# Two weight items of each expert mixture in borrowed memory, and experts laid out by quarters of columns

## What is computed

```python
# first block: 32 experts of width 512, each token has two of them
for e in range(N_EXPERTS):
    h = jax.nn.silu(t @ w_gate[e]) * (t @ w_up[e])
    y = y + combine[:, e:e + 1] * (h @ w_down[e]).astype(jnp.float32)
...
# second block, both layers: 16 experts of width 1024, each takes its 32 best tokens
cap = EC_CAPACITY_FACTOR * n // N_EXPERTS_2
aff = jax.nn.softmax(h.astype(jnp.float32) @ w_router.astype(jnp.float32), axis=-1)
g, idx = lax.top_k(aff.swapaxes(1, 2), cap)
xs = jax.vmap(lambda hb, ib: hb[ib])(h, idx)
a = jax.nn.silu(jnp.einsum('becd,edf->becf', xs, w_gate)) * jnp.einsum('becd,edf->becf', xs, w_up)
y = jnp.einsum('becf,efd->becd', a, w_down) * g[..., None].astype(h.dtype)
...
# around each mixture of the second block
sh_m, sc_m, g_m, sh_f, sc_f, g_f = ada_params(c, ada_w[l], ada_b[l])
x = x + g_m * y
x = x + g_f * ec_moe(modulate(x, norm_ffn[l], sh_f, sc_f), ...)
```

## Time and profile before

| | us |
|---|---|
| median of 3 runs | 2042.81 (2042.49 to 2046.18) |
| the profiled execution | 2041.44 |
| its span, first to last instruction | 2039.4 |
| PE busy | 1616.9 (79%) |
| DVE, ACT, POOL busy | 562.9, 298.1, 88.1 |
| transferred | 711.34 MB, mean 349 GB/s |

### The profile page before, as it was taken

How to read it: one execution, slowest core, us unless ns; L and a number is a source line. 1 busy time by engine, 2 the same in 40 slices (tenths; PEclk the granted TensorE clock), 3 DMA queues, 4 the chain that set the end, 5 groups by cost and what they waited for, 6 DMA issues and landing times.

```text
span 2039.4 us, 21810 instructions
## 1 busy us (share of the span) xinstructions
PE 1616.9 (79%) x8868; PEld 755.1 (37%) x8868; DVE 562.9 (28%) x1055; ACT 298.1 (15%) x707; POOL 88.1 (4%) x102
## 2 busy tenths in 40 slices
PE   7999788888888798896676867666997677767767
PEld 3455544433334244664231313112874132313212
DVE  3753311111111177744111101112653111101101
ACT  2123211111111111332010101001001110100000
POOL 2210000000000052000000000000000000000000
PEclk9989799999999899897888988988997898888988
DMA  9532499999999966434999999999973999999997
GB/s 364 202 128 73 191 422 419 422 421 424 422 422 422 406 232 238 174 145 164 421 419 420 423 420 420 424 420 407 377 298 124 421 420 425 420 420 422 423 421 317
DMA packets 118364, 711.34 MB, mean 349 GB/s; under 512 B 5763, under 2 KB 8067, under 8 KB 93571
## 3 DMA queue, kind: packets, MB, share of 16 engines
...
HBM read 709.03 MB, written 1.05 MB: 348 GB/s over the span
## 4 chain that ended last, share of the span: by engine, by line
DMA 48%; PE 37%; DVE 6%; issue 4%; ACT 3%; POOL 2%; POOLq 0%; ACTq 0%; DVEq 0%
DMA ring<-in_moe_w_down 39%; DMA ring<-in_w_down 8%; PE bank L1475 7%; PE bank L459 4%; PE bank L1430 4%; PE bank L2229 4%; PE bank L1499 4%; PE bank L1348 4%; PE bank L900 1%; PE bank L603 1%; PE bank L2007 1%; POOL small L255 1%; DVE gate_rows L371 1%; DVE ada_acc L371 1%; PE bank L314 1%
## 5 line engine op out<-in xcount | busy, mean ns | idle before, releaser
L1430 PE MATMUL bank<-ring,arena 128*32 128x512 f32 x3072 | 401.8, 651 | 143.3 <-DMA ring<-in_moe_w_up 100.9
L1475 PE MATMUL bank<-ring,arena 128*32 128x512 f32 x1536 | 230.9, 728 | 160.7 <-DMA ring<-in_moe_w_down 121.2
L1499 PE MATMUL bank<-arena 128*128 128x512 f32 x512 | 236.3, 604 | 28.2 <-DVE arena L1554 16.1
L1521 DVE COPY arena<-bank 128x512 f32<-128x512 f32 x96 | 66.4, 691 | 666.0 <-PE bank L1430 666.0
L1430 PEld LDWEIGHTS bank<-ring,arena 128*32 128x32 f32 x3072 | 93.6, 114 | 378.9 <-issue 251.7
L459 PE MATMUL bank<-ring,hT 128*128 128x512 f32 (+1 forms) x352 | 158.6, 602 | 1.6 <-DVE hT L329 1.6
L1475 PEld LDWEIGHTS bank<-ring,arena 128*32 128x32 f32 x1536 | 50.5, 121 | 293.7 <-issue 183.0
L1513 ACT ACTIVATE arena<-bank 128x512 f32<-128x512 f32 x96 | 57.3, 597 | 615.4 <-PE bank L1430 615.4
L1499 PEld LDWEIGHTS bank<-arena 128*128 128x128 f32 x512 | 92.8, 191 | 136.8 <-issue 95.1
L1348 PEld LDWEIGHTS bank<-arena,xn 128*128 128x128 f32 x512 | 124.5, 335 | 8.3 <-DVE arena L1380 3.7
L1348 PE MATMUL bank<-arena,xn 128*128 128x128 f32 x512 | 123.5, 404 | 3.3 <-DVE arena L1380 3.3
...
## 6 DMA issues: line engine op xcount, KB each, us to landing
...
```

The costliest lines, as they stand in the source:

```text
L1430: last = nc.tensor.matmul(AA[hf if M.nf == 2 else up][32 * j:32 * j + 32, :], xgT[:, x + kk, a:a + C], w[:, kq + j, hf * NC:(hf + 1) * NC] ...
L1475: last = nc.tensor.matmul(AA[n][32 * j:32 * j + 32, :], act_s[:, b, q * C:(q + 1) * C], w[:, j, n * NC:(n + 1) * NC], start=(kk < 4), stop ...
L1499: nc.tensor.matmul(Y[2 * t + n][:, :], wselT[:, e % 2, t * P:(t + 1) * P], z_s[:, n * NC:(n + 1) * NC], start=(e == 0 and M.fresh), stop=( ...
L1521: v.tensor_copy((up_s if up else gate_s)[:, a:a + NC], AA[1][:, :]).then_inc(M.u_dve if up else M.g_dve, 1)
```

## The change

- **Lent memory.** Items 4 and 7 of each mixture no longer go to the ring. Item 4 goes to `arena[:, 8192:12288]`, item 7 to the whole of `gate_rows`, each 2 MB. SP waits for the last users of that memory in the dense part (`lent_free`). The ring places of the other items shift down. To make room, `ctxT` moves to `gate_rows`, the gate of the mixtures becomes `gate_strips` (256 columns on four groups of 32 partitions), and some small tiles move.
- **The context** is prepared at the end of M1, at experts 28 to 30 (loads, squares, scale, turns, evacuation by ACT and DVE), in `gate_rows`, instead of in block 1.
- **Quarters of columns.** In M2's gate and up, and in all down products, quarter j of the array now takes 256 of the 1024 output columns and the whole contraction. The items of M2 need 16 matmuls of 256 columns instead of 8 of 512. Copies and sums of gate and up are gone in M2; silu and product read PSUM. z is 256 columns wide. M1's gate and up stay as they were.
- **Return by row groups.** `back_pe` has 8 matmuls of 32 contraction rows and 256 columns, in two halves of four on four row groups and four banks, with a wait between the halves.
- **Gather** goes over four banks; from the second group on it also waits for the product and the turned weights of the expert before.
- **Flag.** It is read ahead of the last four experts of M1 on PE, ACT, DVE; the branch stays behind M1.
- Gate loads from `ada_b`: one of 512 KB at the start of block 2 and of the odd layer each, and 4 small ones (128 KB together) at the start of block 1 and of the odd layer, in place of four of 512 KB.

```diff
+HEAD = 8192
+QW = D // 4
+LENT = (4, 7)
...
-    items += [("moe",)] * (3 * E1)
+    items += [("moe", i) for i in range(3 * E1) if i not in LENT]
...
+            if sec % 6 == G_F:
+                for j in range(4):
+                    last = nc.tensor.matmul(banks[0][32 * j:32 * j + 32, 0:QW], const("ones")[:, 0:C], acc[:, j * QW:(j + 1) * QW],
+                                            start=True, stop=True)
...
         def ctx_load_act():
-            nc.scalar.wait_ge(at_v, 16)
+            nc.scalar.wait_ge(M1.done, M1.done0 + LENT[1] + 1)
...
         def gather_pe(M, k, g, r):
+            if g:
+                pe.wait_ge(M.act, nth(M, GE * g - 1, 1, r, k))
+                pe.wait_ge(M.wT, nth(M, GE * g - 1, 1, r, k))
             for kk in range(KD):
-                if kk >= 2:
-                    pe.wait_ge(M.xg_dve if kk % 2 else M.xg_act, nth_group(M, 4 * g + kk // 2, 4, r, k))
+                if kk >= 4:
+                    pe.wait_ge(M.xg_dve if kk % 2 else M.xg_act, nth_group(M, 4 * g + kk // 2 - 1, 4, r, k))
                 for t in range(T):
-                    last = nc.tensor.matmul(AA[kk % 2][:, 0:GE * C], xn[:, t, kk::KD], sel[:, b * T + t, :], start=(t == 0), stop=(t == T - 1))
+                    last = nc.tensor.matmul(XG[kk % 4][:, 0:GE * C], xn[:, t, kk::KD], sel[:, b * T + t, :], start=(t == 0), stop=(t == T - 1))
...
-                            kk = n * part + kq + j
-                            last = nc.tensor.matmul(AA[hf if M.nf == 2 else up][32 * j:32 * j + 32, :], xgT[:, x + kk, a:a + C],
-                                                    w[:, kq + j, hf * NC:(hf + 1) * NC], start=(kk < 4), stop=(kk >= 4))
+                            last = nc.tensor.matmul(GU[up][32 * j:32 * j + 32, 0:QW], xgT[:, x + kk, a:a + C],
+                                                    w[:, kq, j * QW:(j + 1) * QW], start=(kk == 0), stop=(kk == KD - 1))
...
         def down_pe(M, k, e, r):
-                        last = nc.tensor.matmul(AA[n][32 * j:32 * j + 32, :], act_s[:, b, q * C:(q + 1) * C],
-                                                w[:, j, n * NC:(n + 1) * NC], start=(kk < 4), stop=(kk >= nk - 4))
+                        last = nc.tensor.matmul(z_bank(M)[32 * j:32 * j + 32, 0:QW], act_s[:, b, q * C:(q + 1) * C],
+                                                w[:, kq, j * QW:(j + 1) * QW], start=(kk == 0), stop=(kk == nk - 1))
...
         def back_pe(M, k, e, r):
-            for t in range(T):
-                for n in range(2):
-                    nc.tensor.matmul(Y[2 * t + n][:, :], wselT[:, e % 2, t * P:(t + 1) * P], z_s[:, n * NC:(n + 1) * NC],
-                                     start=(e == 0 and M.fresh), stop=(e == M.ne - 1 and M.gate is not None)).then_inc(M.y, 1)
+            for n, order in enumerate((((0, 0), (0, 2), (1, 1), (1, 3)), ((0, 1), (0, 3), (1, 0), (1, 2)))):
+                if n:
+                    pe.wait_ge(M.y, nth(M, 8 * e + 4, 8, r, k))
+                for t, j in order:
+                    rows_, at = slice(32 * j, 32 * j + 32), (j % 2) * QW
+                    nc.tensor.matmul(Y[2 * t + j // 2][:, at:at + QW], wselT[rows_, e % 2, t * P:(t + 1) * P], z_s[rows_, :],
...
             def put(i, rows_):
                 free(M, k, i, r, looped)
+                if i in M.lent:
+                    n = M.lent.index(i)
+                    nc.sync.dma_start(lent[n].rearrange("p (k n) -> p k n", n=rows_.shape[2]), rows_).then_inc(lent_arrived[n], 16)
+                    return
...
+        def lent_free(stage, n):
+            if stage == 1:
+                return [(at_m, 24), (ada_sums, 4)] if n else [(at_q, 4), (at_v, len(att1))]
+            if stage == 2:
+                return [(out_added, 8)] if n else [(a2_o, 4), (a2_v, len(att2)), (fourier_steps, FY_MM)]
+            return [(out_added, 12)] if n else [(ada_sums, 13)]
```

392 lines of the change are left out of this document (220 added, 172 removed).

## The result

Median 2021.56 us (2020.46 to 2025.22, four runs) against 2044.10 (2042.49 to 2046.18, four runs) of the kernel before: ratio 0.9892, interval 0.9875 to 0.9909. The change gives 22 us where I forecast 42, and the time lies 6.6 us above the upper end of my range. The profiled execution is 2021.36 us with a span of 2019.5.

A forecast was written before the change was run, and what follows sets the result against it. Mixtures were taken as bound by weight transfers not started ahead, dense parts by PE, DVE and small-step chains. From 2041.44 us, -29.8 - 5.4 + 2.5 - 5.5 - 2.5 - 1.0 = -41.7 gave 1999.7, stated as 2001; range 1991 to 2015.

The forecast's parts named there:

- M1's end: From expert 30's down to block 2's first matmul: 17.65 us before, 10.7 to 12.4 forecast; gain taken as 5.5.
- first gathers: Each mixture's first gather, on the path: four banks instead of two save 1.8 us each, 5.4 over three.
- M2[0]'s end: From 1400.31 to the norm: 16.9 us before, 16.5 or 14.8 forecast; gain taken as 1.0.
- context load: Context loads moved into M1's stream of transfers: 1.05 MB at 422 GB/s, 2.5 us lost.
- M2[1]'s end: From expert 14's down to the last addition's end: 18.9 us before, 17.9 or 16.2 forecast; gain taken as 1.5.
- Lending: Two more items transferred ahead of each of three mixtures, 9.94 us each: 29.8 us gained.
- no gain in the middle: M2's items by quarters of columns: 1.93 us of PE each, under the transfers' 5.0, so nothing changes.
- My bound of 0: Lower bound of a first gather's gain (upper 3.9 us): nothing saved if all of it runs at the low clock.
- 3 if the issue stays: At M1's end, the gain is only 3 us if the branch's 3.35 us of issue does not shrink to 1.
- Dense parts: Outside the mixtures: cheaper gate sums gain about 2 us, ACT's issue of five transfers loses 1; together 1 gained.
- Rival 2: Only the transfers gain: PE at low clock, row groups one after another, gathers stay 7.9 us; 2014 us, chance 0.12.

The follow-up runs named there:

- e1: The changed kernel with no item lent, all of a mixture's items through the ring of five: 2051.33 us, ratio 1.0035 to the kernel before.
- e2: The changed kernel with both M2's gate, up and down matmuls issued as before, half as many, numbers not the reference's: 2017.01 us, ratio 0.9870.
- e5: The changed kernel with the gather's weights read from neighbouring columns instead of every eighth, so other features than the reference's: 2014.95 us, ratio 0.9873.
- e12: The changed kernel with the gather over two banks as before, all else as changed: 2022.29 us, ratio 0.9898.
- e14: The changed kernel with ScalarE writing the normed rows a second time by feature, and the gather on neighbouring columns: 2012.69 us, ratio 0.9855.
- e15: The changed kernel with matmuls that keep TensorE busy in its waits and later odd-layer gate loads, the gather's weights still strided: 2013.27 us, ratio 0.9858.
- e8: The changed kernel loading 16 columns of each context row instead of 1024, so block 2's values differ from the reference's: 2024.53 us, ratio 0.9921.
- e4: The changed kernel without the block of further M1 passes for experts with more than 32 tokens; the flag's load stays: 2015.49 us, ratio 0.9861.
- e6: The changed kernel with matmuls only keeping TensorE busy in each mixture's last expert and behind M2[0]'s last return: 2022.38 us, ratio 0.9901.
- e3: The kernel before with do-nothing TensorE instructions added in both M2, which were absent from the program that ran: 2044.04 us, ratio 1.0005.

## Why the prediction was wrong, point by point

On the profiled executions I forecast 41.7 us and got 20.1. The 21.6 us that are missing lie in these steps: instruction fetches, which had no term, 7.2 (0.8 of it not shown); M1's end 5.5; the first gathers 5.4; M2[0]'s end 2.3; the context load 1.0; the lent items 0.8; and M2[1]'s end gave 0.8 more than forecast.

- **Lending**, -29.8: right, -29.0 by e1, or -27.0 if the longer distance in e1's M1 is taken off. SP was in time in all three.
- **Quarters of columns, "no gain in the middle"**: this is the step that failed most, in size and in its reasoning. I costed 32 against 16 instructions an item in PE's time, found 1.93 us under 4.97 and took it as free. That is what it is for PE. But the instructions themselves come through the DMA engines, the one resource that was full: 3.1 and 3.3 us in the two M2 (e2). In M1 I put it at some 0.8, the distance at the end of 4.0 instead of 3.2, with 14 fetches instead of 11; other traces with 14 end at 3.2 to 4.2, so this 0.8 is not shown.
- **First gathers**, -5.4: 0. I read 0.96 us a step as the round trip over two banks at the full clock. It was the strided weight loads (e5, e12, e14). The row to see it by stood in the page of before too, below: 335 ns a load (second row), where other loads of 128 x 128 fp32, those of the return, took 191. That the loads are as busy as the matmuls would not have told it, since they are in e14 too (65.4 and 68.4 us). My bound of 0 was for another reason, the low clock, and that was the second limit (e14, e15).

```profile
L1499 PEld LDWEIGHTS bank<-arena 128*128 128x128 f32 x512 | 92.8, 191 | 136.8 <-issue 95.1
L1348 PEld LDWEIGHTS bank<-arena,xn 128*128 128x128 f32 x512 | 124.5, 335 | 8.3 <-DVE arena L1380 3.7
```

- **Context load**, +2.5: the mechanism right, the size 3.5 (e8).
- **M1's end**, -5.5: 0, 17.68 us from expert 30's down to block 2, where it was 17.65 and my sum at the full clock had 10.7. To the last return's end it is 10.43 instead of 13.38, but I had 8.7: the last down started 6.4 us behind the one before it and not 4.97, since that one ran at the half clock (3.60) and PE's chain behind it, not the landing, came last; and the return was 1.6 where I had 1.3. Then the issue went to 5.5, not to 1, and the closing matmuls took 1.7 at the half clock, not 1.05; "3 if the issue stays" was the bound, and the issue grew. It is the jump (e4).
- **M2[1]'s end**, -1.5: -2.3 (16.6 us instead of 18.9), as the last item and return ran at the full clock.
- **M2[0]'s end**, -1.0: +0.3 up to the norm (1385.21 to 1402.40, 17.2 us instead of 16.9), and +1.3 up to the first transposes. The half clock took 1.5 (e6). And although the return takes 1.6 us at the full clock instead of 3.7, its second half closes all four banks, where before the first token block's two were closed early: the norm began 1.0 us ahead of the return's end (1417.20 in the earlier trace rows, the return ending at 1418.16), and now begins 1.3 behind it.
- The last 1.0 us there is a step of GpSimd between the norm's squares and its scaling (timelines, first before, then changed). It now begins 0.04 us behind VectorE's squares and takes 1.24 us instead of 0.19. At this place it does so in every trace with the changed return (1.23 to 1.24) and in none with the old one; at the start of block 2, where it begins just as close, it takes 1.23 to 1.24 in both kernels. No run moved it by itself.

```profile
1418.44 0.19 POOL L299 TENSOR_SCALAR small<-small 128x1 f32<-128x1 f32 x1 [488.80 <-ACT xn L279]
1418.92 1.22 DVE L290 CUSTOM_DVE_ANT_0 xn<-h 128x1024 f32<-128x1024 f32 x1
...
1403.60 1.23 DVE L297 CUSTOM_DVE_ANT_0 xn<-h 128x1024 f32<-128x1024 f32 x1
1403.64 1.24 POOL L306 TENSOR_SCALAR small<-small 128x1 f32<-128x1 f32 x1 [482.52 <-ACT xn L286]
```

- **Dense parts**, -1.0: -1.6 in block 2 and +1.3 in the odd layer by the means of several traces, -0.3 in sum and within the spread of 3 to 5 us between such traces. The rest of the profile's -4.2 and +3.2 is chance of one execution each.

By stage ahead of the last item, counted from the first gather to the last item's landing (us):

```
          before   after   gained   forecast   missed   named above
M1         463.1   458.0     5.1       9.2      4.1     gather 1.8, context 1.0, fetches 0.8
M2[0]      463.3   456.9     6.4      11.7      5.3     gather 1.8, fetches 3.1, lent items 0.6
M2[1]      463.8   456.6     7.2      11.7      4.5     gather 1.8, fetches 3.3, lent items 0.3
```

The remainders, +0.5, -0.2 and -0.9, are smaller than the 2.0 and 1.3 us by which the same program differs from itself in e3, so they say nothing. Rival 2 (only the transfers gain, 2014) was nearest in kind, and had neither the fetches nor the longer jump.
